# A mixture-of-experts stage on one core: features reordered, rows of four experts gathered already turned, and one expert's weights outside the ring

## The chip, the core and the metric

The kernel is one program on one NeuronCore of a Trainium2 chip. TensorE (PE; PEld is its weight load), VectorE (DVE), ScalarE (ACT), GpSimd (POOL) and SyncE (SP) each run their own instruction stream and meet on semaphores. SP issues the weight transfers, POOL nearly all others; 16 DMA engines move the data. The metric is device time in microseconds of one execution. Three runs of the kernel before took 1739.17, 1744.84 and 1742.44 us, median 1742.44.

## What is computed

Two layers over 384 tokens (128 of context, 256 latent) with 1024 features, all in float32. Each layer has a mixer (layer 0: attention beside a matrix memory; layer 1: neighbourhood attention) and then a mixture of 32 experts, of which each token uses two of one group of eight:

```python
e_logits = (xt @ we + be).reshape(t, N_GROUPS, EXPERTS_PER_GROUP)      # of the chosen group
top_v, top_i = lax.top_k(e_logits, TOP_K_IN_GROUP)
...
def expert_block(args):
    xi, e = args
    hid = jax.nn.silu(xi @ w1[e]) * (xi @ w3[e])        # w1, w3: 1024 x 512
    return hid @ w2[e]                                  # w2: 512 x 1024
```

The change touches this second half of each layer alone, and the norm in front of it. Every expert's three matrices (2 MB each) are read once per layer, so 192 transfers of 2 MB in all.

## The kernel before, in words

**Weights.** SP walks through one list of chunks, `stream`, 2 MB each: modulation, projections, and for each layer `("moe", l, 3 * e + j)`, j = 0, 1, 2 for w1, w3, w2. A chunk lies in slot n % 6 of `ring`. Before chunk n goes out SP waits until chunk n - 6 has been read (`freed`): w1 and w3 at the end of the expert's hidden products (`hid_done`), w2 at the end of its down products (`y_done`). SP stands still at that wait, and everything behind it in the list stands too. `expert_dram` reads w1 and w3 with features p*4+k of the first half and of the second half in partition p, that is two runs of 8 KB per partition; w2 is one run of 16 KB.

**Rows of an expert.** After the norm `h` (L1333, L1334) holds the tokens. The routing on DVE gives `key`, the rank of a token in each expert. For each expert up to 64 rows are gathered by products with a 0/1 matrix `sel` (DVE, `pick`, L1736): `token_products` (L827) puts the rows in PSUM, ACT copies them (L1149), `token_turns` (L833) turns them with four transposes, DVE copies them to `xT` (L1728). `index_products` (L839) finds where each row's result goes, DVE rounds it into `idx` (L1744). So each expert has its own chain, one expert ahead of its use.

**An expert on TensorE.** `hidden_products` (L846, L847; 16 products side by side in two column halves), then the token products of the next expert, `hidden_turns` (L852), the index products and token turns of the next expert, then `down_products` (L859). Beside it ACT applies SiLU (L1159), copies one half of the turned rows (L1164) and the result (L1169); DVE copies the other half of the hidden rows (L1722) and multiplies (L1751); POOL scatters the result to DRAM (L1931). Experts 2 to 29 are a loop of two. A product in float32 shows as two records in the trace.

**POOL's queue.** In each layer it loads gate, shift and scale of the norm and the router's matrices, waits until the mixer's result has been added (`x_mixed`), loads the next gate (`load_G(l, 1)`), waits for the norm (`h_ready`), loads the shift and scale of the next layer (`load_AB(1, 0)`; in layer 1 the final norm's gain), and then issues the 32 scatters.

**The rest.** `weigh` on DVE, after expert 0, computes the tokens' weights and the blocks over 64 rows; with these inputs no expert has more, and the overflow part runs empty.

## Time and profile before

| | |
|---|---|
| median of three runs | 1742.44 us |
| profiled execution | 1743.03 us |
| its span, first to last instruction | 1741.2 us |
| PE busy | 1551.4 us (89%) |
| DVE busy | 446.2 us (26%) |
| ACT busy | 301.9 us (17%) |
| chain that ended last | PE 80%, DVE 8%, DMA 5% |
| read from DRAM | 511.08 MB |
| mean granted TensorE clock | 0.931 of 2.4 GHz |

The page divides the span in 40 slices of 43.5 us. Slices 10 to 20 and 30 to 39 are the expert stages of layers 0 and 1; between them lies layer 1's mixer. Busy tenths of 9 mean 90% and more. The busy time of PE is from modelled ends, so whether it waits is read from the starts of its instructions in the timeline rather than from the share.

### The profile page before, as it was taken

The numbers are of one execution on the slowest core, as the hardware profiler recorded it, in microseconds if no ns is written. First come the engines' busy times: TensorE is split into PE (matmuls) and PEld (weight loads), VectorE is DVE, ScalarE is ACT, GpSimd is POOL, SyncE is SP. The second block draws the span as 40 slices with busy tenths as digits, with TensorE's granted clock in tenths as the row PEclk, the third lists the DMA queues.
The fourth block names the chain that finished last, engine by engine and source line by source line (L and its number), as shares of the span: only waits on it lengthen the run. The fifth ranks groups of instructions, "written<-read, shape, count | busy, mean of one in ns | idle before, by whom it ended". The sixth has DMA issues, their size and how long they took to land.

```text
span 1741.2 us, 21413 instructions
## 1 busy us (share of the span) xinstructions
PE 1551.4 (89%) x8379; PEld 738.7 (42%) x8379; DVE 446.2 (26%) x1067; ACT 301.9 (17%) x614; POOL 146.1 (8%) x200
## 2 busy tenths in 40 slices
PE   6799876787999999999957998896999999999991
PEld 4355764444434334334423444544443343343440
DVE  0030475523311111111123023643311111111113
ACT  3100213411111111111111003421111111111112
POOL 1101102100000000000004000010000000000000
PEclk9899986997999999999987997897899999999996
DMA  9996943105999999999969422023599999999992
GB/s 351 234 357 215 384 147 135 66 18 219 416 424 424 423 423 423 423 424 424 423 250 318 150 97 85 1 77 133 204 422 424 424 424 424 422 424 424 424 393 112
DMA packets 99302, 521.62 MB, mean 300 GB/s; under 512 B 10130, under 2 KB 11610, under 8 KB 56240
## 3 DMA queue, kind: packets, MB, share of 16 engines
q1 hardware_dynamic: 85920, 485.58, 69.0%
q0 software_dynamic: 13328, 35.29, 6.6%
q8 instruction: 38, 0.62, 0.2%
q14 instruction: 16, 0.13, 0.0%
HBM read 511.08 MB, written 20.22 MB: 305 GB/s over the span
## 4 chain that ended last, share of the span: by engine, by line
PE 80%; DVE 8%; DMA 5%; ACT 2%; SPq 2%; issue 1%; POOL 0%; DVEq 0%; POOLq 0%; ACTq 0%
PE psum L846 24%; PE psum L859 13%; PE psum L534 13%; PE psum L827 9%; PE psum L792 5%; PE psum L852 2%; DMA ring<-in_ab_w_in 2%; PE psum L833 2%; PE psum L839 2%; SPq L370 2%; PE psum L458 1%; DMA ring<-in_moe_w 1%; PE psum L707 1%; PE psum L720 1%; PE psum L802 1%
## 5 line engine op out<-in xcount | busy, mean ns | idle before, releaser
L846 PE MATMUL psum<-ring,area_t 128*64 128x512 f32 x1024 | 451.8, 594 | 2.8 <-issue 1.1
L847 PE MATMUL psum<-ring,area_t 128*64 128x512 f32 x1024 | 452.0, 594 | 0.0
L846 PEld LDWEIGHTS psum<-ring,area_t 128*64 128x64 f32 x1024 | 139.8, 137 | 293.9 <-issue 292.2
L859 PE MATMUL psum<-ring,area_t 128*64 128x512 f32 x1024 | 235.5, 602 | 2.2 <-DVE area_t L1751 2.2
L534 PE MATMUL psum<-ring,area_t 128*128 128x512 f32 (+1 forms) x528 | 222.4, 583 | 7.9 <-DMA ring<-in_ab_w_in 7.9
L1722 DVE COPY area_q<-psum 64x512 f32<-64x512 f32 x64 | 44.5, 695 | 571.4 <-PE psum L847 571.3
L827 PE MATMUL psum<-area_h,area_t 128*64 128x512 f32 x768 | 180.1, 604 | 3.0 <-DVE area_t L1736 3.0
L534 PEld LDWEIGHTS psum<-ring,area_t 128*128 128x128 f32 x528 | 101.3, 193 | 125.7 <-issue 115.7
L1931 POOL DMA_INDIRECT pair_rows<-area_q,idx x64 | 62.4, 975 | 941.0 <-ACT area_q L1169 926.5
L847 PEld LDWEIGHTS psum<-ring,area_t 128*64 128x64 f32 x1024 | 139.8, 137 | 0.0
L859 PEld LDWEIGHTS psum<-ring,area_t 128*64 128x64 f32 x1024 | 68.8, 137 | 120.5 <-issue 113.0
L1159 ACT ACTIVATE area_q<-psum 64x512 f32<-64x512 f32 x64 | 37.9, 592 | 407.3 <-PE psum L847 407.3
L827 PEld LDWEIGHTS psum<-area_h,area_t 128*64 128x64 f32 x768 | 57.1, 140 | 113.2 <-issue 109.9
L792 PE MATMUL psum<-ring,area_q 128*128 128x512 f32 x192 | 87.6, 618 | 0.0
L1169 ACT COPY area_q<-psum 128x512 f32<-128x512 f32 x64 | 37.5, 586 | 284.9 <-PE psum L859 284.9
L1751 DVE TENSOR_TENSOR area_t<-psum,area_t 128x256 f32<-128x256 f32 x64 | 27.2, 425 | 182.6 <-ACT area_t L1164 182.6
L1267 DVE COPY area_q<-psum 128x512 f32<-128x512 f32 (+2 forms) x20 | 12.6, 629 | 214.2 <-PE psum L534 202.3
L1149 ACT COPY area_q<-psum 128x512 f32<-128x512 f32 x64 | 37.5, 586 | 136.3 <-PE psum L827 136.3
L852 PEld LDWEIGHTS psum<-keep,area_q 128*128 128x128 f32 x256 | 35.8, 210 | 53.7 <-issue 50.3
L792 PEld LDWEIGHTS psum<-ring,area_q 128*128 128x128 f32 x192 | 37.9, 200 | 46.9 <-issue 46.9
L1728 DVE COPY area_t<-psum 128x512 f32<-128x512 f32 x64 | 44.3, 692 | 31.8 <-PE psum L833 31.8
L1051 ACT COPY area_q<-psum 128x512 f32<-128x512 f32 (+1 forms) x18 | 10.2, 564 | 241.0 <-PE psum L534 234.1
(251 smaller groups left out, 1375.8 us busy)
## 6 DMA issues: line engine op xcount, KB each, us to landing
ring<-in_moe_w SPq DMA_DIRECT2D x192, 2048.0 KB, 15.9
ring<-in_ada_w SPq DMA_DIRECT2D x24, 2048.0 KB, 18.6
ring<-in_na_w_in SPq DMA_DIRECT2D x6, 2048.0 KB, 18.2
ring<-in_ab_w_in SPq DMA_DIRECT2D x5, 2048.0 KB, 24.4
area_m<-mod_ready POOLq DMA_DIRECT2D x6, 1024.0 KB, 9.5
area_q<-pair_rows POOLq DMA_DIRECT2D x6, 1024.0 KB, 7.3
ring<-in_ab_w_out SPq DMA_DIRECT2D x2, 2048.0 KB, 16.0
area_g<-mod_ready POOLq DMA_DIRECT2D x4, 1024.0 KB, 8.0
```

The lines of the kernel that those rows point to most:

```text
L534: mm = pe.matmul(banks[2 + g % 4][:, 0:w], hT[:, k, t * P:t * P + P], wchunk(n, KT)[:, k, 0:w], start=(k == 0), stop=(k == KT - 1))
L792: mm = pe.matmul(banks[2 + g % 2][:, :], qkv[l][:, t, c0 + k * P:c0 + k * P + P], wchunk(n, KT)[:, k, :], start=(k == 0), stop=(k == KT - 1))
L827: mm = pe.matmul(banks[0][64 * half:64 * half + 64, :], pick[:, 0:BLOCK], h[:, t, 512 * half:512 * half + 512], start=(n == 0), stop=(n == ...
L846: pe.matmul(banks[2 + u][0:64, :], lhsT, w1[:, k, :], start=(k == 0), stop=(k == KT - 1))
L847: mm = pe.matmul(banks[2 + u][64:128, :], lhsT, w3[:, k, :], start=(k == 0), stop=(k == KT - 1))
L852: mm = pe.transpose(banks[4][:, k * P:k * P + P], hs[u][:, k:512:4], ident)
L859: mm = pe.matmul(banks[6 + u][64 * j:64 * j + 64, :], hidT[u][:, k, :], w2[:, k, 512 * j:512 * j + 512], start=(k == 0), stop=(k == 3))
L1149: act.copy(tok, banks[0][:, :]).then_inc(M["tok_copied"], 1)
L1159: act.activation(hs[u][0:64, :], banks[2 + u][0:64, :], ACT.Silu).then_inc(M["silu_done"], 1)
L1722: v.tensor_copy(hs[u][64:128, :], banks[2 + u][64:128, :]).then_inc(M["up_copied"], 1)
L1728: v.tensor_copy(xT[u][:, :, :].rearrange("p k s -> p (k s)"), banks[1][:, :]).then_inc(M["xT_copied"], 1)
L1931: pool.indirect_dma_start(out=pair_dram[l], in_=ysb[u], in_offset=None, out_offset=bass.IndirectOffsetOnAxis(ap=idx[u][:, :], axis=0), bou ...
```

## The change

1. *Order of features.* The norm before the experts writes `h` so that feature q*8+k stands at k*128+q (strided writes). All matrices, the router's too, are then read with 8 neighbouring features in a partition: w1 and w3 become one run of 16 KB per partition.
2. *Gather.* `gather(l, q, g)` computes the turned rows of four experts (a quad) directly: a 128x128 piece of `h` is the stationary operand, the selections of four experts (`sel4`, 256 columns) move. A quad takes 24 products of 256 columns in four parts; the first quad of a layer is gathered for two experts at a time, 128 columns. DVE copies each part to `xT4` (`turn`). The table `GATHERS` says behind which expert's hidden products each part stands. Token products, token turns, index products per expert and ACT's token copy go.
3. *Places.* The 32 experts' target rows come from six products once per layer (`places`), from a rank per token (`rank_slots`).
4. *Spare.* w1 and w3 of expert 2 (`SPARE`) leave the list. `load_spare` puts them in `area_m` and `area_g`, which held modulation; POOL's `load_G(l, 1)`, `load_AB(1, 0)` or the gain are issued behind the scatter of expert 2.
5. The loops over experts are written out; `weigh` stands after expert 12.

```diff
+SPARE = 2
...
-            stream += [("moe", l, c) for c in range(3 * EXPERTS)]
+            stream += [("moe", l, c) for c in range(3 * EXPERTS) if c not in (3 * SPARE, 3 * SPARE + 1)]
...
-            w = a["moe_w1" if j == 0 else "moe_w3"][l].rearrange("e (h p k) n -> e p h (k n)", h=2, k=4)
+            k = 4 if j == 2 else KT
+            v = a[("moe_w1", "moe_w3", "moe_w2")[j]][l].rearrange("e (p k) n -> e p (k n)", k=k)
...
+        GATHERS = {0: ((0, 2),), 1: ((0, 3), (1, 0)), 2: ((1, 1), (1, 2)), 3: ((1, 3),)}
+        for _e in range(4, EXPERTS - 4):
+            GATHERS[_e] = ((_e // 4 + 1, _e % 4),)
+        for _e in range(EXPERTS - 4, EXPERTS):
+            GATHERS[_e] = ()
...
+            def load_spare(l):
+                def piece(dst, src):
+                    sp.dma_start(dst, src).then_inc(spare_landed, 16)
+                sp.wait_ge(S["x_mixed"], (l + 1) * NT * OUT_CHUNKS)
+                w3 = expert_dram(l, SPARE, 1)
+                for half in range(2):
+                    piece(spare[1][half], w3[:, 2048 * half:2048 * half + 2048])
+                sp.wait_ge(S["h_ready"], NT * (2 * l + 2))
+                piece(spare[0], expert_dram(l, SPARE, 0))
...
+            def gather(l, q, g):
+                pe.wait_ge(M["sel_ready"], l * PICKS + (1 + g // 2 if q == 0 else 2 + q))
+                n = 4 * (QUADS * l + q) + g
+                if n >= 2:
+                    pe.wait_ge(M["xT_copied"], n - 1)
...
+                for i, k in enumerate(ks):
+                    for t in range(NT):
+                        mm = pe.matmul(banks[n % 2][:, w * i:w * i + w], h[:, t, k * P:k * P + P],
+                                       sel4[q % 2][:, t, cols, :].rearrange("p e s -> p (e s)"),
+                                       start=(t == 0), stop=(t == NT - 1))
...
+                gather(l, 0, 0)
+                gather(l, 0, 1)
+                for e in range(EXPERTS):
...
+                        hidden(l, e, *(lambda k, n=n: wchunk(n, KT)[:, k, :] for n in up))
+                    for q, g in GATHERS[e]:
+                        gather(l, q, g)
+                    if e == 0:
+                        places(l)
+                    turn_hidden(l, e)
+                    n = NUM["moe", l, 3 * e + 2]
+                    pe.wait_ge(landed[place(n)], when(n))
+                    down(l, e, wchunk(n, 4))
...
-                stt(h[:, t, :], x[:, t, :], rstd[:, t:t + 1], modA[:, c, :], ALU.mult, ALU.mult)
-                tt(h[:, t, :], h[:, t, :], modB[:, c, :], ALU.add, "h_ready")
+                if idx % 2:
+                    out = out.rearrange("p (k q) -> p q k", k=KT)
+                    rows, by, plus = (v.rearrange("p (q k) -> p q k", k=KT) for v in (rows, by, plus))
+                stt(out, rows, rstd[:, t:t + 1], by, ALU.mult, ALU.mult)
+                tt(out, out, plus, ALU.add, "h_ready")
...
+                pick(l, 0, 2)
+                pick(l, 2, 4)
+                for g in range(2):
+                    turn(l, 0, g)
+                rank_slots(l)
+                pick(l, 4, 8)
+                for e in range(EXPERTS):
+                    one(l, e)
+                    product(l, e)
+                    for q, g in GATHERS[e]:
+                        turn(l, q, g)
+                    if e % 4 == 0 and e // 4 + 2 < QUADS:
+                        pick(l, e + 8, e + 12)
+                    if e == 0:
+                        index(l)
+                    if e == WEIGH_AT:
+                        weigh(l)
...
-                pool.wait_ge(S["x_mixed"], NT * OUT_CHUNKS * (l + 1))
-                load_G(l, 1)
...
                 for e in range(EXPERTS):
-                    scatter(M, e, e % 2, base, l)
+                    scatter(M, e, e % 2, base, l, idx[:, e:e + 1])
+                    if e == SPARE:
+                        pool.wait_ge(M["y_done"], base + SPARE + 1)
+                        load_G(l, 1)
+                        if l == 0:
+                            load_AB(1, 0)
+                        else:
+                            get(modA[:, 0, :], spread(a["norm_final"]), "gfin_loaded")
```

TensorE between two experts' hidden products, first in the kernel before (inside the loop of experts 2 to 29):

```order
L827 MATMUL psum<-area_h,area_t 64x512 x6
L852 MATMUL psum<-keep,area_q 128x128 x4
L839 ISA
L839 MATMUL psum<-area_q,area_t 128x1
L839 ISA
L839 MATMUL psum<-area_q,area_t 128x1
L839 ISA
L839 MATMUL psum<-area_q,area_t 128x1
L833 MATMUL psum<-keep,area_q 128x128 x4
L859 MATMUL psum<-ring,area_t 64x512 x8
```

and in the changed kernel, experts 4 to 27 (L886 is the gather, L862 the turns of the hidden rows, L869 the down products, L855 and L856 the next hidden products):

```order
L886 MATMUL psum<-area_t,area_h 128x256 x6
L862 MATMUL psum<-keep,area_q 128x128 x4
L869 MATMUL psum<-ring,area_t 64x512 x8
L855 MATMUL psum<-ring,area_q 64x512
L856 MATMUL psum<-ring,area_q 64x512
```

Nothing stands any more between the turns of the hidden rows and the down products.

SP at the start of layer 0's experts, before (L370 ends the projections' chunks, L395 are the experts'; L399 is the loop):

```order
L370 DMA ring<-in_ab_w_out 128x8x512 x2
L395 DMA ring<-in_moe_w 128x2x2048 x2
L395 DMA ring<-in_moe_w 128x4096
L395 DMA ring<-in_moe_w 128x2x2048 x2
L395 DMA ring<-in_moe_w 128x4096
L399 UNCONDITIONAL_BRANCH
```

and now (L379 loads into the ring, L394 into the spare places):

```order
L379 DMA ring<-in_ab_w_out 128x8x512 x2
L379 DMA ring<-in_moe_w 128x4096 x6
L394 DMA area_m<-in_moe_w 128x2048
L394 DMA area_g<-in_moe_w 128x2048
L394 DMA area_m<-in_moe_w 128x4096
L379 DMA ring<-in_moe_w 128x4096 x88
```

Six chunks of experts 0 and 1 go as before, then expert 2's w3 and w1, then the 88 others, each behind the chunk six places ahead of it in the shortened list.

POOL in layer 0, before (L1850 is every plain load, L1931 the scatter):

```order
L1850 DMA area_q<-in_moe_be 128x32
L1850 DMA area_g<-mod_ready 128x2048
L1850 DMA area_m<-mod_ready 128x2048 x2
L1931 DMA pair_rows<-area_q,idx 1536x512 x32
```

and now (L1859 and L1940):

```order
L1859 DMA area_q<-in_moe_be 128x32
L1940 DMA pair_rows<-area_q,cond 1536x512 x3
L1859 DMA area_g<-mod_ready 128x2048
L1859 DMA area_m<-mod_ready 128x2048 x2
L1940 DMA pair_rows<-area_q,cond 1536x512 x29
```

The three loads of 1 MB moved from before the experts to behind the third scatter.

## Rows read from the trace of the kernel before

**Rows 1.** The page, busy tenths in 40 slices of the span.
```profile
PE   6799876787999999999957998896999999999991
...
DMA  9996943105999999999969422023599999999992
```

**Rows 2.** Window in layer 0: length, busy per engine (x), clock, DMA share, GB/s.
```profile
600.00:700.00 100.00, 100.00 (x504) 40.09 (x502) 16.37 (x35) 14.38 (x27) 6.82 (x7) 1.00 1.01 424
```

**Rows 3.** Timeline of one expert on PE: start, length, engine, line, operation.
```profile
613.51 0.59 PE L846 MATMUL psum<-ring,area_t 128*64 128x512 f32 x1
...
620.38 2.75 PE L827 MATMUL psum<-area_h,area_t 128*64 128x512 f32 x12
623.05 0.75 PE L852 MATMUL psum<-keep,area_q 128*128 128x128 f32 x4
...
624.87 3.65 PE L859 MATMUL psum<-ring,area_t 128*64 128x512 f32 x16
628.35 0.59 PE L846 MATMUL psum<-ring,area_t 128*64 128x512 f32 x1
```

**Rows 4.** Timeline, the same expert on DVE.
```profile
624.24 0.42 DVE L1751 TENSOR_TENSOR area_t<-psum,area_t 128x256 f32<-128x256 f32 x1 [2.96 <-ACT area_t L1164]
```

**Rows 5.** Timeline, first hidden product of experts 0, 25, 31; then 0, 28, 31.
```profile
420.56 0.61 PE L846 MATMUL psum<-ring,area_t 128*64 128x512 f32 x1 [0.88 <-DVE area_t L1728]
...
791.57 0.59 PE L846 MATMUL psum<-ring,area_t 128*64 128x512 f32 x1
...
882.23 0.61 PE L846 MATMUL psum<-ring,area_t 128*64 128x512 f32 x1
...
1230.17 1.03 PE L846 MATMUL psum<-ring,area_t 128*64 128x512 f32 x1 [0.94 <-issue]
...
1647.49 0.61 PE L846 MATMUL psum<-ring,area_t 128*64 128x512 f32 x1
...
1692.63 0.61 PE L846 MATMUL psum<-ring,area_t 128*64 128x512 f32 x1
```

**Rows 6.** Chunks' line L395, windows 425:470 and 850:890.
```profile
DMA to landing us min/median/max: 7.9/12.1/14.9
...
DMA to landing us min/median/max: 17.9/19.9/22.4
```

**Rows 7.** DMA issues: count, KB each, median us from issue to landing.
```profile
ring<-in_moe_w SPq DMA_DIRECT2D x192, 2048.0 KB, 15.9
...
area_m<-mod_ready POOLq DMA_DIRECT2D x6, 1024.0 KB, 9.5
```

**Rows 8.** Timeline, products of 272 and of 128 columns with 128x128 stationary.
```profile
172.04 11.27 PE L534 MATMUL psum<-ring,area_t 128*128 128x272 f32 x48
...
203.89 1.95 PE L612 MATMUL psum<-area_t 128*128 128x128 f32 x16
```

**Rows 9.** Timeline from routing to experts, layer 0, and a window there.
```profile
412.49 1.03 DVE L1736 TENSOR_TENSOR area_t<-keep,area_q 128x384 f32<-128x384 f32 x2
...
413.11 5.14 PE L827 MATMUL psum<-area_h,area_t 128*64 128x512 f32 x12 [1.49 <-DVE area_t L1736]
...
419.72 0.69 DVE L1728 COPY area_t<-psum 128x512 f32<-128x512 f32 x1 [6.20 <-PE psum L833]
...
414.00:418.00 4.00, 4.00 (x12) 0.95 (x8) 0.00 (x0) 0.00 (x0) 0.00 (x0) 0.52 0.00 0
```

**Rows 10.** Timeline, last norm step of the third tile, layer 0, and the next turns.
```profile
394.01 1.23 DVE L1254 TENSOR_TENSOR area_h<-area_h,area_m 128x1024 f32<-128x1024 f32 x1
...
396.34 1.95 PE L515 MATMUL psum<-keep,area_h 128*128 128x128 f32 x8
```

**Rows 11.** Window in which mostly w2 moves.
```profile
606.00:613.00 7.00, 7.00 (x40) 3.29 (x38) 2.25 (x5) 1.39 (x3) 0.00 (x0) 1.00 1.01 426
```

**Rows 12.** Window and timeline, last down products of layer 0.
```profile
888.00:892.00 4.00, 2.04 (x12) 0.77 (x9) 1.12 (x2) 0.96 (x2) 0.00 (x0) 1.00 0.42 160
...
891.99 5.35 PE L859 MATMUL psum<-ring,area_t 128*64 128x512 f32 x16 [1.12 <-DVE area_t L1751]
```

## What was predicted

> **What bounds the kernel now.** I read the page's slices first: in two long stretches, which are the two expert layers, TensorE and the DMA engines both show 9 in nearly every slice [rows 1]. A window inside one gives PE 100 us of 100, DMA share 1.01, 424 GB/s [rows 2]. So two resources are full at once, and the question is which one paces. The timeline of one expert answers for most of the layer: hidden products start at 613.51 and again at 628.35, one expert is 14.84 us of TensorE work without a hole [rows 3]. The landing times answer for the rest: from issue to landing a chunk takes 12.1 us at the layer's start and 19.9 us at its end [rows 6], so the transfers fall slowly behind TensorE. The starts of the hidden products [rows 5] show where that ends: layer 0 takes 882.23 - 420.56 = 461.67 us for 31 experts where 31 x 14.84 = 460.0; the last six take 90.66, or 15.11 each, the last three of layer 1 45.14, or 15.05 each. So TensorE paces to about the 25th expert and the weights pace the last ones. Both limits must be redone for the change. I write Y for the start of a layer's first hidden product. The stretch Y to expert 31 is 461.67 us in layer 0 and 462.46 in layer 1.
>
> **TensorE per expert.** Removed per expert: six token products 64x512 (620.38 to 623.05, 2.67 us), three index products and four token turns. Added in a quad's steady state: six gather products 128x256. The row with 272 columns gives (11.27 - 0.40)/47 = 0.231 us per record, two records per product, so 0.46 us, by 256/272 0.435 us, six 2.61 us [rows 8]; 0.40 is its last record's drain. The gather thus costs what the token products did. The index products and turns looked like a saving, but they stood between the turn of the hidden rows (623.05) and the down products (624.87, 1.82 us later) [rows 3]. In that time DVE multiplies from 624.24 to 624.66 [rows 4]; with some 0.15 us to release TensorE (as 420.41 to 420.56 in [rows 5, 9]) the down products could start at 624.81 at the earliest. The cover goes and the wait takes its place: 1.76 us against 1.82. Period: 6.87 + 2.61 + 1.76 + 3.48 = 14.72 us against 14.84.
>
> The first experts cost more. The first quad is gathered in halves of 128 columns: 24 records by (1.95 - 0.28)/15 = 0.111 us [rows 8] are 2.7 us each. Expert 0: 6.87 + 2.7 + 12 records of the places products 1.3 + 1.76 + 3.48 = 16.1. Expert 1 has two gathers, 17.4; expert 2 two of the second quad, 17.3; expert 3 14.7; experts 4 to 27 24 x 14.72 = 353.3; experts 28 to 30 gather nothing, but then wait about 1.05 us for DVE's copy (0.69, as in [rows 9]) and its releases: 13.2 each, 39.5. Sum 458.3 us from Y to expert 31, by TensorE alone; in the last experts the two holes of 1.05 and 1.16 us may lower the clock, as the slow last down products did, up to 1.7 us: 458.3 to 460.
>
> **The transfers.** The ring keeps six chunks and its order; expert 2's w1 and w3 go elsewhere, in time when the DMAs are at 0.00 [rows 9], so these 4 MB are free. But who frees a slot changes. Chunks in order: (2,w2) and (3,w1) at the end of hidden 0, (3,w3) at y 0, (3,w2) and (4,w1) at hidden 1, (4,w3) at y 1, and (4,w2) only when expert 2's w2 is read. With the experts' times above these are Y+6.9, 16.1, 23.0, 33.5 and 50.8. A chunk is 2048 KB at 424 GB/s, 4.95 us [rows 2, 7]; so the six are in at about Y+39.6, and SP stands before (4,w2) until Y+50.8. The engines are idle about 14 us where before they were full. The two chunks loaded ahead are worth 9.9 us; this hole takes them back. The fastest landing was 7.9 us [rows 6], 2.95 more than the transfer; I put 1.2 of it ahead of the first packet and 0.8 between the last packet and a TensorE that waits, so the stream runs on from Y+52.
>
> Just there POOL's moved loads fall: gate, shift and scale (three of 1024 KB, in layer 1 one and a 512 KB gain), formerly issued in the idle routing time. At 424 GB/s they are 7.4 us and 3.7 us; one alone took 9.5 to land, 1024 KB [rows 7], which bounds them from above, 0 from below. In layer 0: (4,w2) with them 12.4, then (5,w1), (5,w3) 9.9, so expert 5 has its weights at Y+75.1 against its need at Y+80.3; in layer 1 at Y+71.4. From then each expert needs three chunks and its scatter: 15.11 or 15.05 by the end of each layer before [rows 5]. The longer runs (16 KB against two of 8 KB) could help: 7 us in which mostly w2 moves, which already has such runs, show 426 GB/s [rows 11] against 424 on the mean [rows 2]. That is 0.5%; I take 0.2% off the mean pace of 15.08, bounds 0 and 1%: 15.05 per expert. Expert 31 starts at Y + 75.1 + 26 x 15.05 = Y+466.4 in layer 0, and Y+462.7 in layer 1. Both lie above TensorE's 458.3 to 460, so the transfers pace the end: +4.7 us against 461.67, and +0.2 against 462.46.
>
> **Before Y.** DVE now builds a first selection in three instructions of 128 elements, about 0.2 us more than one of 384 (1.03 us for two) [rows 9]. TensorE then gathers 2 x 24 records, in layer 0 at clock 0.52 until about 418 [rows 9]: 413.3 to 418.3 for the first (records at twice 0.111), 2.7 more to 421.0, DVE copy 0.7 and release: Y = 421.85 against 420.56, +1.3. The copy of tokens on ACT, index and turns go with the old path. Layer 1 likewise +1.2. The val and pval steps that leave the route were hidden behind the ranks' wait, worth 0. The norm's two steps now write h with 512 bytes between neighbours. No row of before has such a write. The nearest are the same steps, 1.23 us and more for 1024 contiguous elements; the last ends at 395.24, while the next turns start at 396.34 [rows 10], so 1.1 us of slack. At equal speed it costs 0; twice as slow would be +2.5 and +1.4 on the path in each layer. I take the row, 0, and keep 1.4 per layer as upper bound.
>
> Of strided access the Trainium skill ("SBUF — State Buffer", note on SBUF cachelines under "Door 1: The DMA port swizzle") says that a step onto a new 16-byte line pays a penalty, so that fp32 is free only to four elements apart. No row of before shows it; by that rule this write is penalised, and the case with 2.8 us more, below, is the one that holds.
>
> Weighing moves from behind expert 0 to behind expert 12, again into the 12 us (3.48 + 6.87 + 1.76) between two duties of DVE; 0. Straight code instead of a loop: no row shows a branch holding TensorE, 0.
>
> **Sum.** +4.7 + 0.2 + 1.3 + 1.2 = +7.4 us. The profiled execution took 1743.03 (span 1741.2, 1.8 around it), 0.6 above the median 1742.44. So 1750.4 in its terms, 1749.8 in the median's; I predict 1749.5. Within 0.3% means 5.2 us, 1737.2 to 1747.7, about what a measurement of this kernel can tell from no change; the forecast lies just above it.
>
> **Rivals.**
> *TensorE paces throughout.* If the runs of 16 KB give 1% (15.11 to 14.96) and the hole is shorter, expert 5 to 31 takes 389 and TensorE's 459.5 decides: -2.2 and -3.0, +2.5 before Y, together -2.7: 1739.7 by the median. For it: the two limits are some 2% apart. Against: 424 and 426. Chance 0.24.
> *The strided write decides* (slower side). Place: norm of the third tile, DVE, on the way to the last turns; price 2.5 us less 1.1 slack, twice, it decides from 1.45 times the present duration on: 1752.3 at twice. At four times it would be 6.4 us, twice: 1762.3. For: it is a new access. Against: nothing seen. Chance 0.22.
> *The clock falls in every expert.* The new hole of about 1.2 us could drop TensorE to 1.2 GHz each time, as at the layer's end, where the last down products took 5.35 us [rows 12]; a warm group reaches its next product after 3.48 [rows 3], and with the drain of its last record I put the difference at 1.7: x 48 experts = 82 us, 1832. Against: the fall there came after three holes close together (SiLU, copy, product), with TensorE busy 2.04 us of 4 [rows 12]; in the steady expert there is one. Chance 0.03.
> *It doesn't do what it says:* expert 2's weights come late. The last part is issued after the last norm step (395.24 [rows 10]), 4 MB need 10 us, and they are read near 421.9 + 33.5 = 455: no. Chance 0.01.
> The forecast has 0.50, and reaches from 1744 to 1752.
>
> **Numbers.** The range 1738 to 1758 leaves out the clock case, fourfold strides and the far end of the first rival. Faster: some of the first rival, and what could still be better than it, 0.12. Same: its rest, the lower third of the forecast and the last rival: 0.33. Slower: the upper part of the forecast, the strided write, the clock: 0.55.
>
> **What the profile after would show.** Hidden products 14.7 us apart in experts 5 to 20 and 15.05 at the end; a hole of about 12 us in the DMA share near Y+40 in both layers; down products released by DVE's product in every expert; Y at 421.9; chunk landings short at first, over 20 us at the end; norm steps at 1.23 or not. The forecast is wrong if the DMA share has no hole, or if the last experts are not spaced wider than the middle ones.

## The result, and the profile after

The changed kernel took 1759.11 us in the median of 4 runs (1758.29 to 1765.30), the kernel before 1740.81 beside it: ratio 1.0123, interval 1.0101 to 1.0145. (The ratios are estimates from all runs and not the quotient of the two medians, which is 1.0105 here.) Later, beside other runs of the kernel before, it took 1757.16, ratio 1.0083 (1.0060 to 1.0105). So it is about 1% slower, some 14 to 18 us. The forecast was 1749.5 with a range to 1758: the sign was right, and the change forecast, +7.1 us, is half of the smaller and less than half of the larger. The profiled execution took 1758.29, span 1756.5, which is 15.3 more than before.

The page after, busy tenths and rate in the 40 slices of the span. Against [rows 1] look at the DMA row in slices 11 and 30, counted from 1: 7 where before had 9:

```profile
PE   5899876787999999899857998886899999999971
...
DMA  9996942215799999999969422024579999999992
GB/s 350 234 367 216 384 154 103 77 52 233 271 429 427 427 426 427 427 427 428 426 266 313 152 96 84 1 76 191 210 298 428 427 428 426 427 428 427 428 388 111
```

The starts of the first hidden product of expert 0 and 31 in both layers, from the timeline (start, length, engine, line, operation), which answer to [rows 5]:

```profile
420.86 0.61 PE L855 MATMUL psum<-ring,area_q 128*64 128x512 f32 x1 [0.87 <-DVE area_q L1740]
...
892.25 0.61 PE L855 MATMUL psum<-ring,area_q 128*64 128x512 f32 x1
...
1239.90 0.61 PE L855 MATMUL psum<-ring,area_q 128*64 128x512 f32 x1 [0.94 <-issue]
...
1707.81 0.61 PE L855 MATMUL psum<-ring,area_q 128*64 128x512 f32 x1 [1.73 <-issue]
```

Write Y for the first of each layer, as the prediction does, and call the time from there to the start of expert 31 the stretch. Y is 0.30 later than before; Y to expert 31 takes 471.39 (before 461.67); from there to layer 1's Y 347.65 (347.94); then 467.91 (462.46); the tail 48.69 (48.57). Of the +15.3 us, 15.2 lie in the two expert stretches.

Where in them, the window view tells (columns as in [rows 2]: window, length, busy per engine, clock, DMA share, GB/s). The stretch of layer 0 before, and after:

```profile
420.56:440.56 20.00, 20.00 (x98) 8.27 (x100) 8.54 (x37) 2.14 (x4) 1.05 (x1) 1.00 0.58 232
440.56:460.56 20.00, 20.00 (x103) 7.94 (x99) 5.22 (x14) 3.32 (x6) 1.01 (x1) 1.00 1.01 408
460.56:480.56 20.00, 20.00 (x105) 8.36 (x105) 4.11 (x9) 2.81 (x6) 0.97 (x1) 1.00 1.01 423
480.56:500.56 20.00, 20.00 (x101) 7.63 (x98) 2.40 (x5) 2.42 (x5) 1.95 (x2) 1.00 1.02 425
500.56:882.23 381.67, 380.87 (x1898) 153.09 (x1895) 62.00 (x129) 55.03 (x104) 24.35 (x25) 1.00 1.01 423
```

```profile
420.86:440.86 20.00, 18.99 (x98) 9.89 (x100) 5.59 (x15) 1.55 (x3) 0.00 (x0) 0.91 0.61 224
440.86:460.86 20.00, 18.99 (x102) 10.52 (x100) 3.57 (x8) 1.55 (x3) 2.05 (x2) 1.00 0.92 360
460.86:480.86 20.00, 19.03 (x89) 10.11 (x86) 2.48 (x5) 1.72 (x4) 2.65 (x4) 1.00 0.46 170
480.86:500.86 20.00, 18.06 (x86) 9.99 (x87) 4.00 (x9) 2.34 (x5) 1.02 (x1) 1.00 1.01 430
500.86:892.25 391.39, 359.73 (x1640) 171.31 (x1637) 55.14 (x127) 40.26 (x79) 25.32 (x26) 0.99 1.01 427
```

Read only the last column. From Y+60 on each kernel moves bytes at one nearly constant rate until the end, 423 before and 427 after. What is worse after lies in the first 60 us. In the third window the engines stand still; call that the hole:

```profile
466.00:474.00 8.00, 7.03 (x35) 4.28 (x35) 1.62 (x3) 0.55 (x2) 0.00 (x0) 1.00 0.00 0
```

**The account** that follows from it, and that the experiments test: a stretch is its bytes divided by the steady rate, plus what the stream of transfers loses in the first 80 us, while the ring is full and SP waits for TensorE to free slots. The steady rate is that of the middle of the stretch, a little finer than in the rows. Counted from the packets' times, before: 191.3 MB / 423.6 GB/s = 451.5 us, and 10.2 lost. After: 190.6 / 426.9 = 446.6, and 24.8 lost. Layer 1: 450.4 + 12.1, and 442.0 + 25.9. The loss can be had from the rows too: 20 x (1 - 224/427) + 20 x (1 - 360/427) + 20 x (1 - 170/427) = 24.7 us. The sum is true by construction; what is found is where the loss lies, and that almost nothing is lost after Y+80 (0.1 us in layer 0, 0.6 in layer 1). That before, too, the transfers and not TensorE set the rate of 423 is seen from the landings, which fall further and further behind their issues, 12.1 us to 19.9 [rows 6].

### The profile page after: what moved, and what is told of

Read it like the earlier page. It is cut to its first block, busy times and chain, and to the rows that moved or that the text cites. A ratio compares the mean times of both kernels' runs of the same rounds, so it can differ in the third digit from the quotient of the medians.

```text
span 1756.5 us, 18927 instructions
## 1 busy us (share of the span) xinstructions
PE 1493.8 (85%) x7859; PEld 803.0 (46%) x7859; DVE 432.2 (25%) x1009; ACT 264.0 (15%) x550; POOL 146.3 (8%) x200
## 4 chain that ended last, share of the span: by engine, by line
PE 77%; DVE 9%; issue 5%; DMA 4%; ACT 2%; SPq 2%; POOL 0%; DVEq 0%; POOLq 0%; ACTq 0%
PE psum L855 23%; PE psum L869 14%; PE psum L544 13%; PE psum L886 10%; PE psum L802 5%; DMA ring<-in_ab_w_in 2%; PE psum L856 2%; PE psum L862 2%; SPq L379 2%; PE psum L468 1%; PE psum L730 1%; PE psum L717 1%; DVE area_q L1249 1%; DVE area_m L1249 1%; PE psum L753 1%
## 5 line engine op out<-in xcount | busy, mean ns | idle before, releaser
L855 PE MATMUL psum<-ring,area_q 128*64 128x512 f32 x992 | 436.3, 593 | 10.8 <-issue 9.2
L856 PE MATMUL psum<-ring,area_q 128*64 128x512 f32 x992 | 437.0, 593 | 0.0
L869 PE MATMUL psum<-ring,area_t 128*64 128x512 f32 x1024 | 242.3, 615 | 62.0 <-issue 60.0
L855 PEld LDWEIGHTS psum<-ring,area_q 128*64 128x64 f32 x992 | 134.0, 137 | 271.4 <-issue 271.2
L886 PE MATMUL psum<-area_t,area_h 128*128 128x256 f32 (+1 forms) x864 | 186.2, 370 | 3.2 <-DVE area_t L1750 3.2
L886 PEld LDWEIGHTS psum<-area_t,area_h 128*128 128x128 f32 x864 | 149.2, 197 | 63.5 <-issue 45.4
L869 PEld LDWEIGHTS psum<-ring,area_t 128*64 128x64 f32 x1024 | 83.3, 140 | 176.9 <-issue 176.9
L1940 POOL DMA_INDIRECT pair_rows<-area_q,cond x64 | 62.6, 978 | 1061.7 <-ACT area_q L1171 823.3
L856 PEld LDWEIGHTS psum<-ring,area_q 128*64 128x64 f32 x992 | 134.0, 137 | 0.0
L1171 ACT COPY area_q<-psum 128x512 f32<-128x512 f32 x64 | 37.5, 585 | 280.5 <-PE psum L869 280.5
L468 PE MATMUL psum<-ring,cond 128*32 128x128 f32 x1536 | 49.9, 291 | 0.0
L468 PEld LDWEIGHTS psum<-ring,cond 128*32 128x32 f32 x1536 | 45.0, 118 | 6.7 <-issue 5.8
L862 PEld LDWEIGHTS psum<-keep,area_q 128*128 128x128 f32 x256 | 40.0, 205 | 15.9 <-ACT area_q L1162 13.5
## 6 DMA issues: line engine op xcount, KB each, us to landing
ring<-in_moe_w SPq DMA_DIRECT2D x188, 2048.0 KB, 17.9
ring<-in_na_w_in SPq DMA_DIRECT2D x6, 2048.0 KB, 17.9
```

What stands on the lines that cost most here:

```text
L468: mm = pe.matmul(banks[7][32 * j:32 * j + 32, 128 * (c % 4):128 * (c % 4) + 128], cond32[:, k, :], w[:, k, 128 * j:128 * j + 128], start=( ...
L855: pe.matmul(banks[2 + u][0:64, :], turned_rows(k), w1(k), start=(k == 0), stop=(k == KT - 1))
L856: mm = pe.matmul(banks[2 + u][64:128, :], turned_rows(k), w3(k), start=(k == 0), stop=(k == KT - 1))
L862: mm = pe.transpose(banks[4][:, k * P:k * P + P], hs[u][:, k:512:4], ident)
L869: mm = pe.matmul(banks[6 + u][64 * j:64 * j + 64, :], hidT[u][:, k, :], w2[:, k, 512 * j:512 * j + 512], start=(k == 0), stop=(k == 3))
L886: mm = pe.matmul(banks[n % 2][:, w * i:w * i + w], h[:, t, k * P:k * P + P], sel4[q % 2][:, t, cols, :].rearrange("p e s -> p (e s)"), sta ...
```

## The experiments

Each ratio is to runs of the kernel before on the same chip (medians 1742.43 for 1 to 4, 1741.89 for 5 to 8, 1743.20 for 9 to 12).

**1. spare8.** Expert 8 outside the ring in place of expert 2; its loads are still issued ahead of expert 2's w2, and POOL's moved loads go behind expert 8's scatter.

```diff
-SPARE = 2
+SPARE = 8
...
-                    if e == SPARE:
+                    if e == 2:
                         load_spare(l)
```

> The changed kernel with one constant moved: expert 8's w1 and w3 stand outside the ring instead of expert 2's, loaded at the same early moment; POOL's moved loads follow expert 8's scatter. My theory, the blocked slot: in the changed kernel SP stands before expert 4's w2 until expert 2's w2 has been read, and the DMAs are idle some 10 us per layer. Here that slot is freed by expert 2's hidden products, so the hole shrinks to about 3 us; the stretch from the first hidden product to expert 31 (471.4 us in layer 0, 467.9 in layer 1) falls to about 461 in both, where TensorE's own chain stands; in all about -17 us, 1741 to 1744. Rival, the written-out code (its fetches hold back landings): nothing changes, 1757 to 1760. Rival, the work of the new gathers on TensorE: nothing changes either.

1756.46 us, ratio 1.0081 (1.0054 to 1.0108), where 1741 to 1744 was expected; stretches 468.31 and 464.62, not 461. The hole did not go: it moved to Y+136 to 142 (5 us) and the first experts still lost 17 us of stream in 80 us, of 25 in the changed kernel. So holding up (4,w2) costs some 8 us of stream and is not the main loss; that theory fell here.

**2. ring_only.** All chunks in the ring, POOL's loads before the experts.

```diff
-SPARE = 2
+SPARE = -1
...
-            stream += [("moe", l, c) for c in range(3 * EXPERTS) if c not in (3 * SPARE, 3 * SPARE + 1)]
+            stream += [("moe", l, c) for c in range(3 * EXPERTS)]
...
+                pool.wait_ge(S["x_mixed"], NT * OUT_CHUNKS * (l + 1))
+                load_G(l, 1)
```

> The changed kernel with all chunks in the ring again and POOL's loads of gate, shift, scale and gain back before the experts; order of features, gather by quads, places and written-out code stay. The blocked-slot theory: no hole after expert 1, no moved loads, so expert 31 comes when TensorE's own chain allows, about 461 us after the first hidden product in both layers: -17 us, 1741 to 1744, which says that holding two chunks more costs rather than gains. Written-out code as rival: 1757 to 1760, since the code is as long. If the chunks held outside do help by themselves: above 1760.

1756.85 us, ratio 1.0075 (1.0053 to 1.0098); stretches 465.17 and 467.01 where 461 was expected. No hole, and still 3.5 and 4.5 us longer than before. Its windows:

```profile
423.74:443.74 20.00, 18.98 (x98) 9.76 (x100) 5.60 (x15) 1.55 (x3) 0.00 (x0) 0.91 0.60 221
443.74:463.74 20.00, 18.99 (x102) 10.44 (x100) 3.57 (x8) 1.55 (x3) 2.06 (x2) 1.00 0.92 365
463.74:483.74 20.00, 19.03 (x89) 10.12 (x86) 2.49 (x5) 1.72 (x4) 0.97 (x1) 1.00 0.94 363
```

The stream runs at 365 and 363 where before had 408 and 423: experts 0 to 2 take 17.9, 17.5 and 17.3 us (before 14.8 to 14.9 each) and free the ring's slots later. The loss is 17.3 and 18.4 us.

**3. tiny_loads.** POOL's moved loads cut to 8 of 1024 columns; gate, shift, scale and final gain are then mostly left out of the computation.

```diff
-                        load_G(l, 1)
+                        get(modG[:, :, 0:8], spread(modf_dram[l, 5, :, 0:8]), "modG_loaded")
...
```

> The changed kernel with POOL's moved loads cut to 8 columns each (gate, shift, scale and gain are then mostly left out of the computation, so the output is not the reference's). Prices the moved loads alone. My theory: they stand in a full stream, so layer 0 gains 3 MB at 424 GB/s, 7.4 us, and layer 1 1.5 MB, 3.7 us: 1747 to 1750. Rival, they hide in the hole after expert 2: within 2 us of the changed kernel, 1757 to 1759.

1755.66 us, ratio 1.0068 (1.0042 to 1.0094); stretches 466.55 and 466.00. 3.5 and 1.7 MB less to move (8.3 and 3.9 us), but in part they had filled the hole, so the loss rose to 28.2 and 27.9: -4.8 and -1.9 us, where -7.4 and -3.7 were expected.

**4. before_unrolled.** The kernel before with its four loops over experts written out.

```diff
-                with pe.Fori(1, EXPERTS // 2 - 1) as i:
-                    for u in range(2):
-                        one(pe.snap(i * 2 + u), u, False)
+                for e in range(2, EXPERTS - 2):
+                    one(e, e % 2, False)
```

> The kernel before with its loops over experts written out, nothing else. My theory: no change, 1739 to 1743; the extra code is some 16 KB per 30 us on the DMAs. Rival, the code's fetches hold back one DMA engine and with it the landing of every chunk: the spacing of the last experts grows and the time by 5 to 15 us.

1747.02 us, ratio 1.0024 (1.0006 to 1.0042); stretches 463.32 and 464.45. "No change" was wrong, by some 4 us (1 to 7 by the interval). The profiled execution shows 3.6 us more in its stretches: 422.8 and 423.0 GB/s in place of 423.6 and 423.7, and 0.4 and 0.8 MB more. Its total was hardly longer, 1743.15 us against 1743.03, since other parts came out shorter; so that the 3.6 us are the 4 of the median is not shown.

After these four the account was formed, and the next eight had to hold to it.

**5. order_only.** The kernel before with the order of features alone: the third norm step's strided write and w1, w3 in runs of 16 KB.

```diff
-            w = a["moe_w1" if j == 0 else "moe_w3"][l].rearrange("e (h p k) n -> e p h (k n)", h=2, k=4)
+            k = 4 if j == 2 else KT
+            v = a[("moe_w1", "moe_w3", "moe_w2")[j]][l].rearrange("e (p k) n -> e p (k n)", k=k)
...
-                    mm = pe.transpose(banks[1][:, k * P:k * P + P], tok[:, k:512:4], ident)
+                    mm = pe.transpose(banks[1][:, k * P:k * P + P], tok[:, k * P:k * P + P], ident)
```

> The kernel before with the order of h's features alone: w1 and w3 read in runs of 16 KB, the third norm step written in strides, the per-expert token products and loops kept. I write Y for the start of a layer's first hidden product. Account theory: the stretch Y to expert 31 is the bytes moved over the rate, plus what the stream of transfers loses while the ring is full at the start (before: 191.3 MB at 423 GB/s, 452, plus 10). With 427 GB/s in place of 423 it would be 458, but TensorE's 31 x 14.84 = 460.0 then bounds it: -1.7 and -2.5 us; the strided steps cost 0.3 on the path in each layer. Total 1739 (ratio 0.998). Rival, the order itself is what costs (the strided steps with their whole 1.4 us and more in each layer, no gain from longer runs): 1746 or more.

1735.04 us, ratio 0.9969 (0.9952 to 0.9986): this part of the change, alone, makes the kernel faster. Stretches 457.85 and 457.82, each 31 x 14.77: TensorE's period fell by 0.07 as well, which makes 2.2 of the 3.8 and 4.6 us gained; the rest is that the transfers no longer pace the last experts. The last window of layer 0:

```profile
504.80:882.65 377.85, 377.85 (x1898) 148.53 (x1896) 62.01 (x129) 54.96 (x103) 24.36 (x25) 1.00 1.01 428
```

At 428 GB/s the transfers just keep up to the end, and PE has no gap in 377.85 us.

**6. loads_in_hole.** The moved loads wait for the hidden products of expert 2, ahead of its scatter.

```diff
-                    if e == SPARE:
-                        pool.wait_ge(M["y_done"], base + SPARE + 1)
+                    if e == SPARE - 1:
+                        pool.wait_ge(M["hid_done"], base + SPARE + 1)
```

> The changed kernel with GpSimd's moved loads issued one scatter earlier, when expert 2's hidden products are done and not after its down products. Account theory: they then fall into the 10 us in which the DMA engines are idle, and no longer compete with the weights: the stretch Y to expert 31 becomes 471.4 - 7.3 = 464 us in layer 0 and 467.9 - 3.7 = 464 in layer 1, total 1748 where the changed kernel took 1759. Rival, single late landings and TensorE's longer first experts set the end, not the bytes: nothing changes, 1757 to 1759.

1757.65 us, ratio 1.0097 (1.0068 to 1.0127). The total did not show what was expected, 1748. The trace does, in layer 0: 463.34 (expected 464), with 323 GB/s where the hole had 170. Part of that, 1.7 us, is that expert 0 took 16.2 in this execution. In layer 1 only 1.3 us came (466.62; expected 464). This profiled execution reached Y 4.1 us later and crossed the mixer 2.1 slower; the same stretches vary by some us from run to run, also between kernels that are equal there. A gain of 9 us in the stretches, and by the medians (1759.11 and, repeated, 1757.16) none to 1.5, with intervals of 5 us to either side: what this edit is worth in the total stays open.

```profile
465.00:485.00 20.00, 19.03 (x89) 10.92 (x86) 3.01 (x5) 2.14 (x4) 2.67 (x4) 1.00 0.87 323
```

**7. split_ring.** ring_only, with each gather split round the turn of the hidden rows.

```diff
+                    elif len(todo) == 1:
+                        gather(l, *todo[0], part=0)
+                        turn_hidden(l, e)
+                        gather(l, *todo[0], part=1)
```

> The changed kernel with all chunks in the ring and the moved loads back before the experts, as in the ring_only run, and besides each gather split: half before the turn of the hidden rows, half between it and the down products, where TensorE waited 1.0 us for DVE's product. TensorE's period in the middle falls from 14.75 to 13.7. Account theory: in the middle that is worth nothing, since the transfers pace there; but the first three experts shorten from 52.6 to about 48 us, so the ring's slots come free 4.5 us earlier and the stream loses 13 in place of 17.5: 191.2 MB at 427 GB/s, 447.8, plus 13 = 461 in each layer, total 1746 where ring_only took 1757. Rival, TensorE paces most of the stretch: 31 experts 1.0 us faster, the stretch falls under 450 and the total to about 1725. Rival, neither matters: 1757.

1750.92 us, ratio 1.0055 (1.0033 to 1.0077); stretches 466.01 and 463.53, both longer than the expected 461, and in layer 0 longer than ring_only's 465.17 (1.2 MB more moved behind Y there). TensorE's period fell to 13.71 as expected, and in layer 0 it stood at 15.0 from expert 8 on anyway: TensorE no longer paced, and a period 1.0 us shorter did not shorten the stretch by the 31 us that the rival had. But expert 1 took 18.8, not 16.3. The timeline of expert 1, DVE and then PE:

```profile
444.63 1.10 DVE L1764 TENSOR_TENSOR area_t<-keep,area_q 128x256 f32<-128x256 f32 x3 [13.16 <-PE psum L889]
445.64 0.24 DVE L1772 TENSOR_SCALAR cond<-psum,keep 128x32 uint32<-128x32 f32 x1
445.92 0.69 DVE L1740 COPY area_q<-psum 64x512 f32<-64x512 f32 x1
```

```profile
441.64 2.94 PE L889 MATMUL psum<-area_t,area_h 128*128 128x128 f32 x24
446.72 0.72 PE L862 MATMUL psum<-keep,area_q 128*128 128x128 f32 x4 [2.13 <-issue]
447.27 2.75 PE L889 MATMUL psum<-area_t,area_h 128*128 128x256 f32 x12
```

DVE stands in the selection for quad 2 (L1764) until the first quad's last gather is done, and only then copies expert 1's hidden rows (445.92), for which PE waits 2.13 us. The changed kernel has the same order; there a second gather covers it.

**8. split_spare8.** Split gathers, the second quad's one expert later, that selection behind expert 1, expert 8 outside the ring, moved loads at its hidden products.

```diff
+        GATHERS = {0: ((0, 2),), 1: ((0, 3),), 2: ((1, 0), (1, 1)), 3: ((1, 2), (1, 3))}
...
+                    if e == 1:
+                        pick(l, 8, 12)
```

> The changed kernel with split gathers, the second quad's gathers one expert later, expert 8 in place of expert 2 loaded outside the ring, and the moved loads issued when its hidden products are done. Account theory: 4 MB less to move after Y, about 3 MB of moved loads more in layer 0 and 1.5 in layer 1; TensorE at 13.7 us runs ahead of the transfers, so no second hole opens: 190.6/0.427 + 11.5 = 458 us in layer 0, 188.8/0.427 + 11.5 = 454 in layer 1; with +2.5 before Y the total is 1732 to 1735, faster than the kernel before. Rival, the holes in the stream come back in any variant that loads ahead (5 us as in spare8): 1745.

1732.69 us, ratio 0.9952 (0.9935 to 0.9968): faster than both kernels, as the account had it. Stretches 457.16 and 454.41, loss 11.0 and 12.2. The first windows of layer 0 (against 224, 360, 170 of the changed kernel), and a middle expert on PE, in which the down products follow without a gap:

```profile
420.78:440.78 20.00, 20.00 (x112) 10.13 (x114) 5.76 (x16) 1.55 (x3) 1.05 (x1) 1.00 0.61 240
440.78:460.78 20.00, 20.00 (x109) 10.73 (x104) 3.85 (x9) 2.51 (x5) 1.00 (x1) 1.00 0.98 404
460.78:480.78 20.00, 20.00 (x95) 10.33 (x95) 3.78 (x7) 1.55 (x3) 0.97 (x1) 1.00 1.01 430
```

```profile
643.26 1.56 PE L889 MATMUL psum<-area_t,area_h 128*128 128x256 f32 x6
644.66 0.63 PE L862 MATMUL psum<-keep,area_q 128*128 128x128 f32 x4
645.13 1.46 PE L889 MATMUL psum<-area_t,area_h 128*128 128x256 f32 x6
646.52 3.65 PE L869 MATMUL psum<-ring,area_t 128*64 128x512 f32 x16
```

**9. after_again.** The changed kernel once more, unchanged.

> The changed kernel once more, beside the three others of this call: 1757 to 1760, ratio near 1.011. Account theory: stretch Y to expert 31 again about 471 and 468 us, the stream's loss at the start 25 us in each layer. Rival, part of the slowdown was a single run's late landings: 1750 or less.

1757.16 us; stretches 471.13 and 467.97, loss 24.8 and 25.8. Ratio as above, a little under the expected 1.011. Not a run's chance.

**10. split_only.** As 8, but all chunks in the ring (the edit of 2).

> As split_spare8, but with nothing loaded outside the ring and the moved loads before the experts as in the kernel before: what the spare expert is worth once TensorE is no longer the bound. Account theory: 191.3 MB at 427 GB/s, 448.0, plus 11 to 12 us of loss = 459.5 in each layer, against 457.2 and 454.4: total 1738 to 1741. Rival, the loads ahead are worth their full 9.8 us per layer: 1752. Rival, they are worth nothing: 1733.

1743.35 us, ratio 1.0006 (0.9990 to 1.0022); stretches 458.92 and 460.03 against the 459.5 expected, total 2 us above. It differs from ring_only only in where gathers and selections stand, and its stretches are 6.3 and 7.0 us shorter. Beside 8, the spare expert is worth 1.8 and 5.6 us in the stretches (about 0.5% of the total), neither its full 9.8 per layer nor nothing: its bytes are partly given back by the moved loads.

**11. split_spare2.** As 8, but with expert 2 outside.

```diff
-SPARE = 8
+SPARE = 2
```

> As split_spare8, but with expert 2 outside the ring, as the change has it, and the moved loads when its hidden products are done. Account theory: the stream is held up until expert 2's down products, now about Y+45 in place of Y+53, and the moved loads fill part of the hole; loss about 15 in layer 0 and 18 in layer 1, so 190.6/0.427 + 15 = 461 and 188.9/0.427 + 18 = 460: total 1741. Rival, which expert is taken decides nothing once TensorE is quicker: 1733.

1743.94 us, ratio 1.0011 (0.9995 to 1.0028); stretches 459.85 and 459.84, loss 13.5 and 17.7. The account was right within 1.5 us per term; total 3 us above. Beside 8, the held-up slot of expert 2 costs 2.5 and 5.5 us of loss even with TensorE quicker.

**12. order_unrolled.** order_only with the loops written out (edits of 4 and 5).

> The order_only kernel with its four loops over experts written out. In before_unrolled the stretch was 1.7 and 2.0 us longer and its total 4 us. Account theory: written-out code lowers the stream's rate by 0.2% through instruction fetches; with 427 GB/s the stream keeps up with TensorE's 14.77 us, so the stretch grows by 1 us at most: total 1735 to 1738. Rival, written-out code costs 4 us or more for another reason (fetches that hold up engines outside the stretch): 1739 to 1741.

1739.35 us, ratio 0.9979 (0.9961 to 0.9997), beside order_only's 0.9969; stretches 459.79 and 459.74, 1.9 us longer each, at 426.7 and 427.0 GB/s in place of 427.8 and 427.9. Expected was 1 us at most. The 2 us per layer is shown twice (4 and 12). The totals don't decide between the two theories: 1739.35 itself lies in the rival's range.

The traces say more of how written-out code costs this. The page's larger instruction queue counts 38 fetches of 16 KB before and 69 with the loops written out; in a stretch there are 3 or 4 against 16 to 19. The added 0.3 MB is 0.7 us at 427 GB/s. The rest may be late landings: from Y+85 on a chunk lands 4.9 us (median) behind the one before it. In the eight profiles with written-out loops whose landings are all recorded and in which no chunk beyond Y+85 lies outside the ring, 19 of 1209 such gaps are over 5.9 us, and a fetch of 16 KB starts inside every one of the 19, though only 222 of the 1209 have one. In the two kernels with loops, none of 300 gaps is over 5.5 us. That the fetches make the landings late is the likely reading; how they do it is not shown.

**What became of the eight expectations.** For the stretches the account was right within 1.5 us in both layers in four of them: 8, 9, 10 and 11. It missed in 5 (460.0 expected, 457.8 came, since TensorE's period fell), in layer 1 of 6 (by 2.6), in 7 (by 5.0 and 2.5) and in 12 (1 us expected, 1.9 came). Of the totals 8 and 9 lay in the range given; the others were off by 1 to 5 us, and 6 by 10.

**The change, part by part**, by stretches in layer 0 and layer 1 (each the difference of two profiled executions; the changed kernel's two lie within 0.3 us of each other, but a fall of the clock in expert 0, told below, can move a stretch by up to 1.7, and the kernel before had one in layer 1, where expert 0 took 16.6 us):

| part | runs compared | layer 0 | layer 1 |
|---|---|---|---|
| order of features | order_only - before | -3.8 | -4.6 |
| written-out loops | order_unrolled - order_only | +1.9 | +1.9 |
| gathers of quads, places, `weigh` later | ring_only - order_unrolled | +5.4 | +7.3 |
| spare expert and moved loads | changed - ring_only | +6.2 | +0.9 |
| all | | +9.7 | +5.5 |

## Why the prediction was wrong in size

**The step that failed is "The transfers"**, with the stretches at Y+466.4 and Y+462.7. They were 471.39 and 467.91: +5.0 and +5.2. The mechanism forecast, a stream held up before (4,w2) and then pacing the end, is what happened; what failed is the size of three terms, by 2.2, 1.6 and 1.2 us in layer 0 and 2.1, 1.9 and 1.2 in layer 1:

- *The release of (4,w2)*, put at Y+50.8, was Y+52.96. Expert 0 was put at 16.1 us and took 17.9; from there every release is 2 us late. Its down products took 5.34 us where the group took 3.65 in [rows 3]. The window view over them, and the timeline:

```profile
431.00:434.00 3.00, 1.99 (x16) 1.76 (x17) 0.94 (x2) 0.37 (x1) 0.00 (x0) 0.94 0.98 421
434.00:438.00 4.00, 4.00 (x14) 1.29 (x12) 0.09 (x1) 0.00 (x0) 0.00 (x0) 0.62 1.01 434
```

```profile
430.66 1.42 PE L896 MATMUL psum<-area_q 128*128 128x32 f32 x12
431.92 0.71 PE L862 MATMUL psum<-keep,area_q 128*128 128x128 f32 x4
433.64 5.34 PE L869 MATMUL psum<-ring,area_t 128*64 128x512 f32 x16 [1.01 <-DVE area_t L1766]
```

TensorE was busy 1.99 of 3 us before them and the granted clock was 0.62 in the next four, a mean of the full 2.4 GHz and the half; compare the 5.35 us in [rows 12]. The prediction weighed this fall for all experts and for the layer's end. At the end it came (5.35 us in experts 28 and 30 of layer 0 and 28 of layer 1), where the transfers pace; but it came in expert 0 too, behind the short places products. With that order it came there in 10 of the 12 layers profiled (17.9 us). In the other two expert 0 took 16.2, the 16.1 of the sum, so the fall is the whole of this miss. With the gap filled it came in none of 8 (15.1).

- *From there to expert 5's weights*: put at 24.3 us behind the release, measured 25.9 (w3 landed at Y+78.9, put at Y+75.1); in layer 1 put at 20.6, measured 22.5 (Y+71.4 and Y+75.4).
- *The pace*: 26 experts at 15.05 = 391.3 were 392.5, though the middle pace was 15.00 to 15.02: a single late landing (16.58 between experts 19 and 20; 16.33 in layer 1) took most of the rest, and the first of the 26, in which the moved loads were still under way, 0.6. In layer 1 the same: 392.5 against 391.3.

**What bounds the kernel** was read too loosely. "TensorE paces to about the 25th expert" is true of the starts, but the rate is at 423 GB/s from Y+40 on (windows above), so the transfers were never ahead: the ring's lead was being used up all the time. Seen so, all that delays the first experts is paid at the end. The prediction counted the longer first experts (17.4, 17.3) in TensorE's own sum of 458.3 to 460 and in the release times, and never asked what they alone cost the stream; that is what most of the +5.4 and +7.3 of the table is laid to, since experiment 10, with shorter first experts, takes 6.3 and 7.0 back. So the prediction had the six chunks in at Y+39.6, and the last of them landed at Y+45.9.

**The runs of 16 KB** were put at +0.2%, bounds 0 and 1%; measured 423.6 to 427.8, +1.0%. The upper bound was the truth. Part of it went to the written-out loops, a term put at 0, which left 427. That 26 experts came within 1.2 us of the 391.3 forecast is partly luck: the rate was higher than put, and the loops and the late landing, neither of them in the sum, took it back.

**TensorE per expert** was right: put at 14.72, measured 14.75; 17.4, 17.3 and 14.7 for experts 1 to 3, measured 17.46, 17.34, 14.75. The gap did take the place of the cover. From the groups of instructions, idle time before the down products (0.97 us each), and one middle expert:

```profile
L869 PE MATMUL psum<-ring,area_t 128*64 128x512 f32 x1024 | 242.3, 615 | 62.0 <-issue 60.0 <-DVE area_t L1766 2.0
```

```profile
646.56 0.42 DVE L1766 TENSOR_TENSOR area_t<-psum,area_t 128x256 f32<-128x256 f32 x1 [2.97 <-ACT area_t L1166]
...
647.08 3.65 PE L869 MATMUL psum<-ring,area_t 128*64 128x512 f32 x16 [0.97 <-issue]
```

The profile names DVE as the releaser for 2.0 of the 62.0 us alone. That it is DVE's product everywhere, as the prediction said, is read from the times: the product ends at 646.98, the down products start at 647.08.

**Before Y** +1.3 and +1.2 were expected, +0.3 and -0.3 came. The strided write was a rival here. The timeline of the third norm's two steps and the turns after them, against [rows 10] and the first of the two steps before:

```profile
392.69 1.28 DVE L1261 SCALAR_TENSOR_TENSOR area_h<-x,small,area_m 128x1024 f32<-128x1024 f32 x1
```

```profile
391.45 1.99 DVE L1256 SCALAR_TENSOR_TENSOR area_h<-x,small,area_m 128x1024 f32<-128x1024 f32 x1
393.47 1.91 DVE L1249 TENSOR_TENSOR area_h<-area_h,area_m 128x1024 f32<-128x1024 f32 x1
```

```profile
395.44 1.97 PE L525 MATMUL psum<-keep,area_h 128*128 128x128 f32 x8
```

The steps took 1.99 and 1.91 us where they took 1.28 and 1.23, 1.55 times; the prediction's sum had them at equal speed. That failed, and the slack hid it. The turns now start 0.06 us behind the last step; before they stood 1.1 behind it. So the slack of 1.1 took nearly all of it, as the threshold of 1.45 said, and some 0.3 us is left on the path. By the rule of the Trainium skill ("SBUF — State Buffer", note on SBUF cachelines under "Door 1: The DMA port swizzle") such a write pays a penalty; the trace agrees, with 0.7 us on each step of 128 x 1024 elements.

**The rivals.** "TensorE paces throughout" is refuted for the changed kernel: layer 0 was at 15.0 from expert 15 on, layer 1 from expert 28 on, and the stretches are 11.4 and 7.9 us above 460, the top of TensorE's own sum. With the order alone it is what happened (experiment 5). "The clock falls in every expert": no, in three of layer 0 and two of layer 1. "It doesn't do what it says": no. The stated sign, a hole of about 12 us near Y+40, came as 10 us at Y+44 to Y+54 in both layers (nothing at all moved for 8 of them). The sum: +7.4 was forecast in the profile's terms and +15.3 came: 10.2 more in the stretches, 2.4 less before Y and around. So the total, too, has an error of 2.4 us on the lucky side.

## What to carry to other kernels

Where two resources are both full, count bytes over rate plus the time in which the stream stands still, over the whole stage; here, with a buffer of fixed size and a stream at its full rate to the end, delays of the consumer in the first 60 us came back as delays of the end. Data loaded ahead is a gain only if the consumer frees the buffer in time: with the gathers split the spare expert gave 0.5% (experiment 8 against 10), in the order as changed nothing or less (the changed kernel against 2). And take a change apart: here one part alone was 0.3% faster, while the whole was 1% slower.

## What was not expected of the hardware

- Runs of 16 KB in place of two of 8 KB in each partition raised the core's steady rate from 423.6 to 427.8 GB/s (1.0%), or, in all twelve profiles with such runs, to 426.7 to 427.9, against 422.8 to 423.7 in the two without.
- Writing loops out lowered it by 0.2 to 0.3% and added 0.3 to 0.8 MB in a stretch, some 0.3 MB of it code: 2 us in 460.
- Two steps on VectorE that write float32 with 512 bytes between neighbours (the second also reads so) took 1.55 times as long as contiguous ones. What the read adds was not tested apart.
- The granted clock can fall behind a gap of 1 us: TensorE was busy 1.99 of 3 us, then the clock was 0.62 over 4 us, and a group of products took 5.34 us in place of 3.65.
- Single landings come 1.4 to 1.7 us late in a steady stream, in the changed kernel and its repeat at the same expert (19 to 20 in layer 0, 27 to 28 in layer 1). All 19 found in eight profiles have a fetch of 16 KB of code in the gap, and kernels with loops have none.
